# A differential-attention loop: the second projection moved to the end of its step, the first made whole at its start in some steps

## The reference

```python
dq = rope(rms_norm(dq.reshape(B, T, DA_HEADS, 2, DA_DK), lp['g_qn']), pos)
dk = rope(rms_norm(dk.reshape(B, T, DA_HEADS, 2, DA_DK), lp['g_kn']), pos)
...
s = jnp.einsum('bqhmd,bkhmd->bhmqk', q, k, preferred_element_type=jnp.float32) * (DA_DK ** -0.5)
if mask is not None:
    s = jnp.where(mask, s, jnp.finfo(jnp.float32).min)
p = jax.nn.softmax(s, axis=-1)
a = p[:, :, 0] - lam * p[:, :, 1]
return jnp.einsum('bhqk,bkhe->bqhe', a.astype(v.dtype), v)
```

## Time and profile before

| | us |
|---|---|
| median of 3 runs | 2151.39 (2151.34 to 2151.4) |
| the profiled execution | 2156.33 |
| its span, first to last instruction | 2154.5 |
| TensorE busy in the span | 2142.9 (99%) |
| VectorE, ScalarE, GpSimd busy | 1161.8, 846.9, 505.6 |
| mean granted TensorE clock | 0.999 of full speed |

### The profile page before, as it was taken

One profiled execution on the slowest core, in us unless ns is written; L12 is line 12 of the kernel. 1 busy time (PEld: TensorE's weight loads), 2 busy tenths in 40 slices (PEclk: granted clock), 3 DMA queues, 4 the chain that ended last, 5 costly groups with the idle time before them and its releaser, 6 DMA issues.

```text
span 2154.5 us, 34910 instructions
## 1 busy us (share of the span) xinstructions
PE 2142.9 (99%) x13462; PEld 2025.9 (94%) x13462; DVE 1161.8 (54%) x2354; ACT 846.9 (39%) x1951; POOL 505.6 (23%) x276
## 2 busy tenths in 40 slices
PE   9999999999999999999999999999999999999999
PEld 9999877789899898998999999999999999999999
DVE  6211544456636556366135648888988982322432
ACT  5200333335546566465312124444344353434411
POOL 5422201230040400501350510000000007576520
PEclk9999999999999999999999999999999999999999
DMA  8522223230040310402942421222222267666211
GB/s 272 199 84 89 62 69 102 78 107 25 26 124 30 89 57 29 122 28 65 325 154 73 149 89 40 82 76 74 90 80 70 80 195 237 189 183 192 88 43 51
DMA packets 319908, 227.18 MB, mean 105 GB/s; under 512 B 17402, under 2 KB 310892, under 8 KB 319757
## 3 DMA queue, kind: packets, MB, share of 16 engines
q1 hardware_dynamic: 222106, 119.68, 19.2%
q10 hardware_dynamic: 97650, 105.46, 14.5%
HBM read 164.47 MB, written 60.62 MB: 104 GB/s over the span
## 4 chain that ended last, share of the span: by engine, by line
PE 95%; issue 1%; DVE 1%; DMA 1%; ACT 1%; POOL 0%; ACTq 0%; DVEq 0%; POOLq 0%
PE ps L838 27%; PE ps L839 27%; PE ps L840 27%; PE ps L1126 3%; PE ps L1102 3%; PE ps L979 1%; PE ps L978 1%; PE ps L1117 1%; PE ps L1049 1%; PE ps L1054 1%; PE ps L1262 1%; PE ps L1051 1%; PE ps L1067 0%; PE ps L1278 0%; POOL w_all L812 0%
## 5 line engine op out<-in xcount | busy, mean ns | idle before, releaser
L838 PE MATMUL ps<-a_hi,w_all 128*128 128x352 f32 (+1 forms) x1360 | 415.6, 306 | 4.8 <-DVE a_lo L2700 4.0
L840 PE MATMUL ps<-a_hi,w_all 128*128 128x352 f32 (+1 forms) x1360 | 413.1, 304 | 0.0
L838 PE MATMUL ps<-a_hi,w_hi 128*128 128x352 f32 x1240 | 405.6, 327 | 0.0
L840 PE MATMUL ps<-a_hi,w_lo 128*128 128x352 f32 x1240 | 397.6, 321 | 0.0
L839 PE MATMUL ps<-a_lo,w_hi 128*128 128x352 f32 x1240 | 397.5, 321 | 0.0
L839 PE MATMUL ps<-a_lo,w_all 128*128 128x352 f32 (+1 forms) x1200 | 368.1, 307 | 0.0
L736 POOL TENSOR_SCALAR w_hi<-w_raw 128x1024 fp32r<-128x1024 f32 x92 | 100.8, 1096 | 967.3 <-DVE scr L2354 447.6
L838 PE MATMUL ps<-w_hi,a_hi 128*128 128x384 f32 (+1 forms) x768 | 286.4, 373 | 0.0
L840 PE MATMUL ps<-w_hi,a_lo 128*128 128x384 f32 (+1 forms) x768 | 273.4, 356 | 0.0
L839 PE MATMUL ps<-w_lo,a_hi 128*128 128x384 f32 (+1 forms) x768 | 272.8, 355 | 0.0
L838 PEld LDWEIGHTS ps<-a_hi,w_all 128*128 128x128 f32 x1360 | 256.1, 188 | 5.8 <-DVE a_lo L2700 4.3
(11 more groups left out here) (285 smaller groups left out, 3571.1 us busy)
## 6 DMA issues: line engine op xcount, KB each, us to landing
w_raw<-w_in SPq DMA_DIRECT2D x64, 512.0 KB, 4.3
w_raw<-w_down SPq DMA_DIRECT2D x48, 512.0 KB, 3.8
raw_half<-w_up SPq DMA_DIRECT2D x80, 256.0 KB, 3.0
hid_d<-scr ACTq DMA_DIRECT2D x22, 512.0 KB, 2.7
w_raw<-w_down SPq DMA_DIRECT2D x24, 384.0 KB, 3.8
scr<-gates_d ACTq DMA_DIRECT2D x24, 352.0 KB, 6.2
gates_d<-full ACTq DMA_DIRECT2D x13, 528.0 KB, 2.6
xt_d<-full ACTq DMA_DIRECT2D x1, 4224.0 KB
```

Of the source, the lines that this page charges most:

```text
L838: pe.matmul(out, lhs[0], rhs[0], start=start, stop=False)
L840: return pe.matmul(out, lhs[1], rhs[0], start=False, stop=stop)
```

## The change

Three things are moved; nothing is added to the computation or taken from it. On TensorE, the second projection goes from its place before the turn to the end of the step, behind the norm transposes. The first projection is done whole, all 8 contraction blocks, at the start of the step, unless the step scores a long row; in those steps (6, 7 and 8 of a head) it stays split in 3 and 5. On VectorE, the copy of the second A transposes goes ahead of the memset and the maximum of scores 1.

```diff
--- before.py
+++ after.py
@@ -1183,7 +1183,10 @@
                     if i >= 2:
                         pe.wait_ge(S["d_rope"], 2 * (n - 1))
                         pe.wait_ge(S["d_v"], n - 1)
-                    project(2 * (i % 2), i, PA_SLOT, PA_SLOT + 3, k1=EARLY)
+                    early = EARLY if scored and not short(scored[1]) else KT
+                    last = project(2 * (i % 2), i, PA_SLOT, PA_SLOT + 3, k1=early)
+                    if early == KT:
+                        last.then_inc(S["pa_done"], 1)
                 if fill and fill[1] == 0:
                     gate_half(fill[0], 0)
                 if scored:
@@ -1203,7 +1206,7 @@
                     if scored:
                         pe.wait_ge(S["d_ev"], 2 * (n + 2))
                     transpose_a(i, 0, min(4, every)).then_inc(S["at0_tr"], 1)
-                if now:
+                if now and (not now[2] or scored and not short(scored[1])):
                     h, i, n = now
                     project(2 * (i % 2), i, PA_SLOT, PA_SLOT + 3, k0=EARLY).then_inc(S["pa_done"], 1)
                 if fill:
@@ -1238,17 +1241,6 @@
                     elif n >= 1:
                         pe.wait_ge(S["e1_done"], n)
                     scores(1, i).then_inc(S["s1_done"], 1)
-                if now:
-                    h, i, n = now
-                    if i == 0:
-                        pe.wait_ge(S["w_split"], 8 * h + (U_DIFF + 7))
-                        if h:
-                            wait_piece(pe, h - 1, 3, S["gate_ev"])
-                        else:
-                            pe.wait_ge(S["gate_ev"], GATE_PIECES)
-                    if n == 1:
-                        pe.wait_ge(S["ot_ev"], RET_TILES)
-                    project(2 * (i % 2) + 1, i, PB_SLOT, PB_SLOT + 3).then_inc(S["pb_done"], 1)
                 if fill:
                     h, k = fill
                     gate_fill(h, 2 * k + 1)
@@ -1278,6 +1270,17 @@
                         last = pe.transpose(ps[:, 7, (2 + m) * P:(2 + m) * P + r],
                                             o_n[0:r, i % 2, m * P:(m + 1) * P], ident[0:r, 0:r])
                     last.then_inc(S["dot_tr"], 1)
+                if now:
+                    h, i, n = now
+                    if i == 0:
+                        pe.wait_ge(S["w_split"], 8 * h + (U_DIFF + 7))
+                        if h:
+                            wait_piece(pe, h - 1, 3, S["gate_ev"])
+                        else:
+                            pe.wait_ge(S["gate_ev"], GATE_PIECES)
+                    if n == 1:
+                        pe.wait_ge(S["ot_ev"], RET_TILES)
+                    project(2 * (i % 2) + 1, i, PB_SLOT, PB_SLOT + 3).then_inc(S["pb_done"], 1)
 
             for p in range(1, 72):
                 branch_piece(p)
@@ -2451,6 +2454,11 @@
                     rotate(ps[0:r, 2 * b, :], i, b, 4, S["d_ropem"], 3 * n, S["d_rope"])
                 if normed and not turned:
                     inverse_of_sum(*normed)
+                if weighed and 4 <= weighed[1] < LAST:
+                    h, i, n = weighed
+                    dve.wait_ge(S["at1_tr"], h * 4 + (i - 3))
+                    dve.tensor_copy(a_t[:, 4:i + 1, :],
+                                    ps[:, 4, 0:(i - 3) * P].rearrange("p (b n) -> p b n", n=P)).then_inc(S["at1_ev"], 1)
                 if scored:
                     h, i, n = scored
                     r, b = rows(i), i % 2
@@ -2458,11 +2466,6 @@
                     hide_last_chunk(1, scored)
                     dve.tensor_reduce(st[0:r, 26 + b:27 + b], score_rows(1, i), axis=AX_X, op=ALU.max,
                                       negate=True).then_inc(S["m1_done"], 1)
-                if weighed and 4 <= weighed[1] < LAST:
-                    h, i, n = weighed
-                    dve.wait_ge(S["at1_tr"], h * 4 + (i - 3))
-                    dve.tensor_copy(a_t[:, 4:i + 1, :],
-                                    ps[:, 4, 0:(i - 3) * P].rearrange("p (b n) -> p b n", n=P)).then_inc(S["at1_ev"], 1)
                 if scored and not short(scored[1]):
                     combine(scored)
                 if turned:
```

## The result

| | before | after |
|---|---|---|
| median of the runs, us | 2151.39 | 2235.78 (2231.37 to 2236.07) |
| ratio, 95% interval | | 1.0379, 1.0366 to 1.0392 |
| span of the profiled execution | 2154.5 | 2234.0 |
| TensorE busy in it | 2142.9 | 2164.9 |
| mean granted TensorE clock | 0.999 | 0.992 |

What follows compares the result with a forecast made beforehand. The prediction took saturated TensorE to bound the kernel. Four heads of 15.5 waits, 0.4 for step 8, less 0.4 saved, gave +62, and the clock +3: 2216 us from 2151.39, range 2202 to 2238.

Steps and rivals of the forecast that it cites:

- What bounds the kernel: Differential attention stage: TensorE is busy throughout each head without slack, so any wait it is given is paid in full.
- The second projection last and the first whole and first: Steps 1 to 5: the turn loses its cover and late scores 0 delay VectorE's rotation; waits of 15.5 us a head.
- The 0.2 for the restart: At the turn, after TensorE waits for the rotation: 0.2 us added to start again, between 0.08 and 0.44.
- what the joined projections were to save: Second and first projection running on from step to step: about 7 beginnings a head fall away, 0.4 us.
- Steps 6 to 8: Long-row steps with the split kept: step 7 covered by half a microsecond, step 8 waits some 0.4 us.
- another microsecond: Turn of steps 7 and 8: the further hold if VectorE's copy stayed behind the maximum of scores 1.
- In the fill steps a gate product of about 4 us stands before the turn, so nothing waits there.: Fill steps of each head: the gate product ahead of the turn covers the chain, so no wait was counted.
- I take a fall in two of the four heads, +3.: TensorE clock after step 2's wait: falls to half, about 1.5 us each time, in two heads, +3 us.
- The first rival: The clock falls after most waits of steps 2 to 5: 16 times 1.5 us, +24, 2237 us; chance 0.20.
- The other rivals: At the turn: only the second projection's lost cover counts, 2177 us, chance 0.07; rotation covered after all, 2150 us, 0.05.
- the lost cover alone: Steps 1 to 4: scores 0 do not hold VectorE, waits 6.3 us a head, +25, 2177 us; chance 0.07.
- the main case: Whole kernel: waits of the turn plus a few clock falls give 2205 to 2226 us; chance 0.68.

Runs made afterwards that it cites:

- the kernel with the clock full: Changed kernel with 18, 12, 9 and 9 extra matmuls, their result thrown away, between scores 1 and the turn in steps 2 to 5: 2222.34 us.
- the experiment with scores ahead: Changed kernel with scores 0 and the A transposes put ahead of the whole first projection in steps that score a short row: 2173.99 us.
- the late steps alone: Order of before in steps 0 to 5 of a head, second projection last only in steps 6 to 8, first projection split throughout: 2162.68 us.
- the sample tile early: Changed kernel with only the sample tile's second projection (step 8 of each head) put back ahead of the turn: 2227.53 us.
- the kernel with the split everywhere: Changed kernel with the first projection split in 3 and 5 blocks in every step again, the second projection still last: 2179.33 us.
- the first two experiments: Changed kernel with the first projection split in every step, 2179.33 us; kernel before with only the first projection whole and first in short-row steps, 2169.03 us.

## Why the prediction was right, and where it was short

*What bounds the kernel.* Right. TensorE had no wait to lose in this stage, and every wait that the change made was paid.

*The second projection last and the first whole and first.* Right in mechanism and in size. The working by steps gave waits of 1.9, 4.1, 3.6, 3.1 and 2.8 in steps 1 to 5. Measured against before they are 1.96 (39.83 - 42.05 + 4.18), 4.13, then 3.67 and 3.18 (from the kernel with the clock full), and 2.70: 15.6 a head against 15.5. The 0.2 for the restart was about right: the chain shows 0.04 and a turn of 0.66 in place of 0.44. These differences already hold what the joined projections were to save, 0.4 a head; no run shows that term by itself. The two experiments with one part each tell the parts apart: alone they cost 27 and 17 us, and taken back out of the change the late scores give 57 and the late second projection 67. Neither is the larger part by itself; some 40 of the 84 us arise only where both stand together, as the prediction's chain had it, and the experiment with scores ahead shows that the late scores act through VectorE.

*Steps 6 to 8.* Right: steps 6 and 7 kept their length within 0.05, and step 8 lost 13.96 - 12.12 - 1.39 = 0.45, forecast 0.4. That the copy on VectorE is needed and free is shown by the two runs on it, at 1.5 to 1.7 in place of "another microsecond".

*"In the fill steps a gate product of about 4 us stands before the turn, so nothing waits there."* This step failed, and the sum had no term for it. The turn does not wait there, but others do. In step 9 ScalarE first copies the sample's second half (line 1679, 1676 before), VectorE adds it, and only then come the memset of scores 0, the copy for the weighing and, behind ScalarE's roots, the exponentials that scores 1 need. With the second projection last, this begins after the turn, the weighing and the norm transposes of step 8. The timeline of the changed kernel, ScalarE, VectorE and TensorE in step 9 of head 0:

```profile
592.70 0.79 ACT L1679 COPY scr<-ps 32x768 f32<-32x768 f32 x1 [2.33 <-PE ps L979]
...
596.77 0.11 DVE L2365 MEMSET ps<- 64x64 f32 x1
...
599.13 1.99 PE L1126 MATMUL ps<-full 128*128 128x256 f32 x8 [0.28 <-DVE full L2428]
...
602.05 1.98 PE L1102 MATMUL ps<-full,scr 128*128 128x512 f32 x4 [0.60 <-ACT scr L1755]
```

and of the kernel before, the copy and the memset in the same step:

```profile
571.72 0.79 ACT L1676 COPY scr<-ps 32x768 f32<-32x768 f32 x1 [0.39 <-PE ps L979]
...
576.91 0.11 DVE L2362 MEMSET ps<- 64x64 f32 x1 [1.09 <-PE ps L1102]
```

Before, VectorE waited 1.09 us for scores 0 here; now scores 0 have ended, at 596.29, when VectorE comes out of the fold (the sum of the sample's two halves) at 596.77. TensorE then stands idle for 0.28 ahead of the weighing, which waits for VectorE's copy, and for 0.60 ahead of scores 1, which wait for ScalarE's exponentials. Counted from the turn of step 8, and without the 2.78 of the 16 matmuls, the weighing begins 0.46 and scores 1 1.23 later than before. Step 9 is 19.64 - 15.58 - 2.78 = 1.28 longer, 5.1 us in four heads. The runs with the late steps alone and with the sample tile early put the loss there and take it away again.

*"I take a fall in two of the four heads, +3."* The mechanism was right and the term too small, in number and in price. The clock fell twice in each head, behind the waits of step 2 and of step 3. The windows of the changed kernel in head 0, columns as in the earlier trace rows:

```profile
494.90:499.20 4.30, 0.44 (x4) 0.25 (x3) 3.82 (x12) 0.46 (x2) 0.00 (x0) 1.00 0.09 30
499.90:503.30 3.40, 3.40 (x13) 3.40 (x12) 1.43 (x6) 1.73 (x4) 0.00 (x0) 0.50 0.11 39
503.50:506.90 3.40, 3.40 (x22) 3.40 (x21) 0.00 (x0) 1.20 (x8) 0.00 (x0) 1.00 0.00 0
509.90:513.40 3.50, 1.62 (x7) 0.81 (x5) 2.90 (x11) 0.56 (x2) 0.00 (x0) 1.00 0.11 37
513.60:514.70 1.10, 0.00 (x0) 0.00 (x0) 1.07 (x3) 0.00 (x0) 0.00 (x0) 0.50 0.00 0
514.90:520.30 5.40, 5.40 (x19) 5.40 (x20) 2.36 (x8) 2.42 (x6) 0.00 (x0) 0.50 0.07 24
```

The second projection behind the wait of step 2 runs at half clock, 13 matmuls in 3.4 us where the next 3.4 us have 22. In step 3 the clock falls while TensorE still waits, and 5.4 us of work follow at 0.50. The first of these cost 9 matmuls or 1.6 us, as forecast; others cost more. Against the kernel with thrown-away matmuls, whose clock was full, steps 3 and 4 are 1.4 to 2.8 us longer in the four heads, 2.0 on the mean of eight falls. The sum is 13.4 by the medians and 15.7 by these steps, where the term had 3. The first rival was therefore about half true, 13 to 16 us in place of its 24: after steps 4 and 5 the clock stayed up.

The Trainium skill (TensorE: Matmul & The Clock Gate, Loop structure matters more than you think) shows a loop with a long wait for a DMA ahead of every matmul as the one in which TensorE goes cold and the matmul behind the wait runs cold. The trace agrees for the waits of steps 2 and 3 of the changed kernel, though it is VectorE that is waited for there. It does not bear out the prediction's wider reading, that every wait would be followed by a slow burst: behind the waits of steps 4 and 5, 3.2 and 2.7 us, the clock stayed up, and in the kernel with the split everywhere, where the longest wait of the turn is 2.1 us, it was 1.0 through the stage.

So the sum reads 4 x (15.6 + 0.45 + 1.28) = 69.3 for waits and 13 to 16 for the clock, 83 to 85 of the measured 84; the forecast had 62 and 3. The other rivals fell with the first two experiments: the chain was not covered, and the lost cover alone, 25 us in that rival, is what the split version costs (27, with the 5 of step 9).

*The signs and the range.* The turn's waits came as named, 24 with the longest at 4.1, and the memset of scores 0 in the chain of step 2 begins 4.5 us after `pb_done` (495.20, against 494.90 less the 4.18 of the first projection). A head takes 161.9 us and not 155 to 156, for step 9 and the clock. The measured time lies outside the main case, 2205 to 2226, and in the range only because that took in most of the clock's case. There is some luck in it: the waits of steps 1 to 5 were forecast, but most of the 20 us beyond the likeliest time are the 5 of step 9, which stood in no term, and a price of the clock of four to five times its term.

## What to carry to other kernels

Where one engine is saturated and another's chain must come back to it, look at what stands between the chain's start and its return on the saturated engine: that work is the cover, and moving it behind the return costs its length less the slack, the time by which the other chain was early, even though nothing is added. (In step 3 that is 4.24 less 3.42, and 0.2 for the restart; with the split everywhere 1.05 was measured.) Look also at which instruction of the other engine stands first in its order: work that is put ahead of its input delays all that is queued behind it, whether it needs that input or not. When waits of some microseconds arise on TensorE, ask for the clock's price too: here the waits of steps 2 and 3 paid 1.4 to 2.8 us each time, those of steps 4 and 5 nothing.

## What was not expected of the hardware

That the wait of step 3 brings the clock down in each head. It is not one idle time: the weighing and scores 1 lie in it (0.80 us idle ahead of them, 2.44 behind), and TensorE was busy for 1.62 of the 3.5 us before the clock went to 0.50. And that 192 matmuls whose result nobody reads pay for themselves, 13.4 us, by keeping the clock at its upper level.
